# Two transformer blocks in one kernel: a 192-byte address step moved from the gated tile to the last low weight tile, and steps moved at the two feed-forward exits

## The chip, the cores and the metric

One core of a Trainium2 chip runs the whole program in one launch. The metric is the device time of one execution in microseconds, the median of several runs. Lower is better.

## What is computed

The reference chains two blocks on 256 tokens of width 1024, in float32.

```
# first block
h = x
h = h + 0.5 * swiglu(rmsnorm(h), ffn1_w1, ffn1_w3, ffn1_w2)      # inner width 2816
z = rmsnorm(h) @ w_in                                            # q, keys, values, gates, u
h = h + concat([nsa_attention(z...), s5_mixer(u...)]) @ w_out
h = h + 0.5 * swiglu(rmsnorm(h), ffn2_w1, ffn2_w3, ffn2_w2)
h = h + sigmoid(rmsnorm(h) @ w_ple_gate) * (p @ w_ple)
x = rmsnorm(h)
# second block, two layers, with 256 context tokens beside the 256 of x
for l in range(2):
    h, hc = modulated norms of x and ctx
    retention, chunk MLP and differential attention from h @ w_in[l]
    out = (sum of sigmoid(merge_logits) * (branch @ w_branch_out[l])) @ w_out[l]
    x = x + gate * rmsnorm(out)                                  # ctx likewise in layer 0
```

`s5_mixer` is a linear state-space scan; its tables of sines and cosines come from the parameters alone.

## The kernel before

Every engine has its program written out by hand, with semaphores between them. There is no scheduler: an engine does its steps in the order of the code.

**Weights.** They come in units of 128 x 1024 numbers (512 KB), in one stream, by SyncE's DMAs into a ring of four slots. A unit is used at nearly full precision in three passes on TensorE (PE). ScalarE (ACT) rounds it to `w_hi` (line 1329), VectorE (DVE) computes `w_lo = ring - w_hi` in `low_part` (line 478). Activations are split the same way, `hn_hi` and `hn_lo`, in the feed-forward parts also `hid_hi` and `hid_lo`. PE then does, for each of the eight 128-column tiles of a unit, `w_hi*x_hi` and `w_hi*x_lo` (`high_passes`, line 558), and after all eight tiles the eight `w_lo*x_hi` (`low_pass`, line 563). Where x is not ready in time the three stand together for each tile (`exact`, line 571). One such matmul moves 256 columns (512 in layer 0 of the second block, where context tokens ride along). The weight tile of the next matmul is loaded (PEld) while one runs.

**Addresses.** `w_lo` lies on the ring's own memory. Each slot has 128 numbers (`PLACE`) of room ahead of it, and `set_back` writes the split parts of some kinds of units 48 numbers (192 bytes) earlier. So for those units the weight tiles start at a multiple of 512 bytes, while `hn_hi` and `hn_lo` start 192 bytes past one. Units of other kinds have both at 192. The hidden tiles have four slots, f % 4: slot 0 of `hid_lo` starts at a multiple of 512 bytes, slots 1 to 3 are moved by `TILE_STEP` = 48 numbers (class `SteppedTiles`) and start 192 bytes past one, and so does every slot of `hid_hi`, which lies behind.

**A feed-forward part** (`ffn`, for `ffn1` and `ffn2`) has 22 steps f, each with a unit of w1, of w3 (`up`) and of w2 (`down`), in the order w1(f+1), w3(f+1), w2(f). The outputs of `down` build up in PSUM banks 0 to 3 over all f. Then PE waits at the exit: DVE adds the four banks to the residual `h` (line 2105), ACT squares the eight tiles of `h` (line 1311), PE sums the squares with a matrix of ones (`sumsq`, line 586, in float32), ACT takes the root (lines 1317 and 1318), DVE scales (line 1932), ACT rounds to `hn_hi` (line 1404), DVE makes `hn_lo` (line 1936), and the next products start.

**Filling work.** After `ffn1` PE has `lags` (line 694) and `turn_input` (line 683, eight transposes a call) for the state-space part; after `ffn2` it has `embedding` (line 984). DVE's `turn_tables` makes the arguments of the tables at f = 5 and 6 of `ffn1`. ACT takes their sines after `ffn1` (lines 1420 and 1421), loads the table of functions for the root (`root_table`, line 1306), and rounds two units. Modulation vectors are matrix-vector products on DVE, two halves of 1024 numbers each (`modulation`, lines 1958 and 1962), strewn over the program.

```
            root_table()
            high_parts(2)
            squares(1, h, resid_ready, [k // 2 + 1 for k in range(KT)])
            root(1, bank(7, 0, T), T, sumsq_ready, 2, D, rstd_ready)
            hn_high(1)
```

## Time and profile before

| | |
|---|---|
| median of 3 runs | 1483.34 us (1478.86 to 1489.1) |
| the profiled execution's own time | 1488.34 us |
| its span in the profile | 1486.6 us |
| PE, DVE, ACT busy | 97%, 64%, 49% of the span |
| PE's granted clock over the span | 0.996 of full |
| HBM read | 220.94 MB |

The profile is of one execution that took 5.0 us more than the median of the runs. The span is the time from the first to the last instruction, 1.74 us less than the execution's own time.

### The profile page before, as it was taken

The page shows a single profiled execution, that of the slowest core. Times are in us where ns is not written, and L with a number is a line of the kernel's source. Part 1 is how long each engine was busy: PE and PEld are TensorE (multiplying, and loading weights), DVE is VectorE, ACT ScalarE, POOL GpSimd, SP SyncE. Part 2 cuts the span into 40 slices and gives each one's busy share as a digit, 9 for nine tenths or more (in the row PEclk, how much of TensorE's full clock was granted, in tenths as well). Part 3 has the DMA queues.
Part 4 walks back from the last instruction along what each step waited for, and adds up shares of the span by engine and source line. Part 5 has one row for each costly group of instructions (what it writes and reads, how often), then busy time and mean ns, then how long its engine had stood idle before and what let it go on. Part 6 is the DMA issues. An engine that isn't in the chain of part 4 may idle for free.

```text
span 1486.6 us, 25861 instructions
## 1 busy us (share of the span) xinstructions
PE 1438.4 (97%) x9976; PEld 1283.5 (86%) x9976; DVE 957.2 (64%) x1516; ACT 721.2 (49%) x1252; POOL 95.7 (6%) x153
## 2 busy tenths in 40 slices
PE   6999999989999998999999999999999999999997
PEld 6999989769999998877778788888889887889997
DVE  5888779677666678865654447654246745646665
ACT  5444465366444466346445353222245446555444
POOL 4700000000000000102001000000000102010000
PEclk9999999999999999999999999999999999999999
DMA  7766645526766744642321224543333542335663
GB/s 279 248 212 202 220 132 197 172 70 232 227 214 221 229 154 152 190 153 78 86 83 60 71 72 156 170 127 114 101 112 100 156 124 83 100 93 184 206 211 130
DMA packets 72440, 227.43 MB, mean 153 GB/s; under 512 B 7072, under 2 KB 21408, under 8 KB 71840
## 3 DMA queue, kind: packets, MB, share of 16 engines
q1 hardware_dynamic: 54528, 194.67, 40.5%
q10 hardware_dynamic: 16416, 27.34, 5.7%
q0 software_dynamic: 1408, 4.20, 1.2%
q8 instruction: 61, 1.00, 0.3%
q14 instruction: 27, 0.22, 0.1%
HBM read 220.94 MB, written 1.05 MB: 149 GB/s over the span
## 4 chain that ended last, share of the span: by engine, by line
PE 83%; DVE 6%; DMA 5%; ACT 4%; issue 2%; SPq 0%; DVEq 0%; ACTq 0%
PE ps L558 33%; PE ps L571 21%; PE ps L563 17%; DMA ring<-stream 4%; DVE w_lo L478 2%; ACT w_hi L1329 2%; PE ps L586 2%; PE ps L1079 1%; PE ps L1095 1%; PE ps L1087 1%; PE ps L1163 1%; PE ps L1152 1%; PE ps L1132 0%; DMA pk<-pack 0%; PE ps L1112 0%
## 5 line engine op out<-in xcount | busy, mean ns | idle before, releaser
L478 DVE TENSOR_TENSOR w_lo<-ring,w_hi 128x1024 fp32r<-128x1024 f32 (+1 forms) x347 | 414.6, 1201 | 267.0 <-ACT w_hi L1329 262.6
L1329 ACT ACTIVATE w_hi<-ring 128x1024 fp32r<-128x1024 f32 (+1 forms) x347 | 360.5, 1040 | 325.1 <-DMA ring<-stream 245.9
L558 PE MATMUL ps<-hn_hi,w_hi 128*128 128x256 f32 (+1 forms) x1720 | 489.3, 315 | 3.6 <-ACT w_hi L1329 1.7
L558 PE MATMUL ps<-hn_lo,w_hi 128*128 128x256 f32 (+1 forms) x1720 | 480.4, 309 | 0.0
L558 PEld LDWEIGHTS ps<-hn_hi,w_hi 128*128 128x128 f32 x1720 | 323.5, 188 | 26.9 <-issue 5.3
L558 PEld LDWEIGHTS ps<-hn_lo,w_hi 128*128 128x128 f32 x1720 | 323.5, 188 | 19.4 <-issue 0.7
L563 PE MATMUL ps<-hn_hi,w_lo 128*128 128x256 f32 (+1 forms) x1720 | 288.5, 310 | 0.5 <-DVE w_lo L478 0.5
L563 PEld LDWEIGHTS ps<-hn_hi,w_lo 128*128 128x128 f32 x1720 | 244.7, 188 | 20.1 <-DVE w_lo L478 0.7
L1398 ACT ACTIVATE area<-ps 128x512 f32<-128x512 f32 (+1 forms) x136 | 67.1, 507 | 192.0 <-PE ps L563 177.9
L571 PE MATMUL ps<-area_r,w_hi 128*128 128x256 f32 (+1 forms) x578 | 132.3, 323 | 1.2 <-ACT area L1398 0.7
L571 PEld LDWEIGHTS ps<-area_r,w_hi 128*128 128x128 f32 x578 | 96.3, 189 | 10.8 <-DVE w_lo L478 0.9
L571 PE MATMUL ps<-area_r,w_lo 128*128 128x256 f32 (+1 forms) x289 | 93.0, 322 | 0.0
L558 PE MATMUL ps<-hid_hi,w_hi 128*128 128x256 f32 x352 | 83.2, 278 | 2.1 <-ACT w_hi L1329 1.3
L558 PE MATMUL ps<-hid_lo,w_hi 128*128 128x256 f32 x352 | 83.0, 278 | 0.0
L571 PE MATMUL ps<-w_hi,hn_hi 128*128 128x512 f32 (+1 forms) x192 | 77.1, 401 | 0.0
L571 PE MATMUL ps<-w_lo,hn_hi 128*128 128x512 f32 (+1 forms) x192 | 73.5, 383 | 0.0
L571 PE MATMUL ps<-w_hi,hn_lo 128*128 128x512 f32 (+1 forms) x192 | 73.2, 381 | 0.0
L558 PEld LDWEIGHTS ps<-hid_hi,w_hi 128*128 128x128 f32 x352 | 66.1, 188 | 2.6 <-ACT w_hi L1329 1.7
L558 PEld LDWEIGHTS ps<-hid_lo,w_hi 128*128 128x128 f32 x352 | 66.2, 188 | 0.0
L571 PE MATMUL ps<-hn_hi,w_hi 128*128 128x256 f32 (+1 forms) x175 | 55.6, 318 | 5.0 <-DVE hn_lo L1936 2.9
L571 PEld LDWEIGHTS ps<-area_r,w_lo 128*128 128x128 f32 x289 | 54.4, 188 | 4.4
L2800 POOL DMA_DIRECT2D area<-area x24 | 14.1, 595 | 683.1 <-ACT area L1398 683.1
(331 smaller groups left out, 1845.5 us busy)
## 6 DMA issues: line engine op xcount, KB each, us to landing
ring<-stream SPq DMA_DIRECT2D x359, 512.0 KB, 3.8
mod_at<-mod_stream ACTq DMA_DIRECT2D x24, 512.0 KB, 5.5
area<-mod_stream ACTq DMA_DIRECT2D x22, 512.0 KB, 4.7
area<-area POOLq DMA_DIRECT2D x16, 128.0 KB, 5.2
area<-area POOLq DMA_DIRECT2D x8, 256.0 KB, 4.0
pk<-pack ACTq DMA_DIRECT2D x1, 1610.0 KB, 7.3
pk<-pack SPq DMA_DIRECT2D x1, 1549.0 KB, 12.0
h<-x_in SPq DMA_DIRECT2D x1, 1024.0 KB, 4.8
```

Source lines behind the costliest of these rows:

```text
L478: eng.tensor_tensor(lo[:, 0:w], raw, hi[:, 0:w].bitcast(F32), ALU.subtract).then_inc(lo_ready[who], 1)
L558: m = pe.matmul(dst, weights[0][wcols], x[n][xcols], start=(start and n == 0), stop=False, skip_group_check=True)
L563: return pe.matmul(dst, weights[1][wcols], x[0][xcols], start=False, stop=stop, skip_group_check=True)
L571: m = pe.matmul(dst, w_, x_, start=(start and n == 0), stop=(stop and n == 2), skip_group_check=True)
L586: m = pe.matmul(bank(b, 0, tokens), c("ones"), src, start=(k == first), stop=(k == KT - 1), skip_group_check=True)
L1079: pe.matmul(bank(4 + m_, T * st, 2 * T - T * st), diffz[rows, 4 + hh, q0:q0 + P], diffz[rows, hh, keys], start=True, stop=True).then_inc(s ...
L1087: m = pe.transpose(bank(6, P * kt, P), aux[:, 4 + n % 2, P * kt:P * kt + P], c("ident"))
L1095: m = pe.matmul(bank(7, P * qt, P), diffv[:, kt, P * hh:P * hh + P], aux[:, 6 + n % 2, P * kt:P * kt + P], start=(kt == 2 * st), stop=(kt ...
L1152: m = pe.matmul(bank(4 + n % 2, T * kt, T), retz[:, hh, T * st + P * kt:T * st + P * kt + P], retz[:, 4 + hh, T * st:T * st + T], start=(k ...
L1163: m = pe.matmul(bank(6 + n % 2, 0, T), retv[:, 2 * st + kt, P * hh:P * hh + P], aux[:, n % 2, T * kt:T * kt + T], start=(kt == 0), stop=(s ...
L1329: act.activation(w_parts(name)[0][:, 0:w], ring[:, u % RING, PLACE:PLACE + w], ACT.Copy).then_inc(hi_ready, 1)
L1398: act.activation(dst, bank(BANK[name][0], 0, tokens), func, **kw).then_inc(act_evac, 1)
```

## The change

**The step.** The class `SteppedTiles` goes, and `hid_hi` and `hid_lo` change places, so that every hidden slot starts 192 bytes past a multiple of 512; everything behind them keeps its address. Instead `low_step` gives 48 numbers for chosen units: all 44 w2 units, units 0 and 4 of `wout` and of `pleg`, and in layer 1 of the second block units 0 and 2 of `dq`, `rq`, `dg`, `rg`, `mu`, `mg`, units 0, 2, 4 and 6 of `wo`, the 8 `mlog` units of branch 0 and the 8 wide `wbo` units. These are 80 units of 347. In such a unit the last of the eight `w_lo` tiles lies 192 bytes further on (`SteppedLow`), 192 past a multiple of 512 like the moving tile. The seven tiles ahead of it stay. DVE makes its `w_lo` in two instructions, of 896 and 128 columns; the second tells PE.

**The exits.** PE adds to a semaphore `bank_down` in the last low pass as banks 0, 1 and 2 are done, and DVE starts each of the first three residual additions on that; the fourth still waits for the whole unit. At `ffn1` the two copies of masks stand ahead of the additions; at `ffn2` one half of a modulation vector is moved behind them. `turn_input(0)` moves ahead of `sumsq(1)`. The two sines move into `ffn1`, to f = 9 and f = 11. Four semaphores become two (`dve_handed`, `act_handed`), with the same order of events.

```diff
@@ -21,7 +21,7 @@
 P = 128
 AREA = 25472
-AREA_SHIFT, TILE_STEP = 32, 48
+AREA_SHIFT = 80
 D = 1024
 KT = D // P
 T = 256
@@ -116,6 +116,31 @@
     return 0
+def low_step(name):
+
+    kind, l = name[0], name[1] if len(name) > 1 else 0
+    if kind in ("ffn1", "ffn2"):
+        return 48 if l == "w2" else 0
+    if kind in ("pleg", "wout"):
+        return 48 if name[1] % 4 == 0 else 0
+    if kind in ("dq", "rq", "dg", "rg", "mu", "mg", "wo") and l == 1:
+        return 48 if name[2] % 2 == 0 else 0
+    if kind in ("mlog", "wbo") and l == 1:
+        return 48 if name[2 if kind == "mlog" else 3] == 0 else 0
+    return 0
+
+
+class SteppedLow:
+
+    def __init__(self, rows, step):
+        self.rows, self.step = rows, step
+
+    def __getitem__(self, at):
+        p, cols = at
+        step = self.step if cols.start >= UW - P else 0
+        return self.rows[p, cols.start + step:cols.stop + step]
+
+
 UNIT_WIDTH = lambda name: BW if name[0] == "wbo" and name[3] == 1 else UW
 SPLIT_UNITS = [name for name in UNITS if name[0] in SPLIT_KINDS]
 SPLIT = {name: n for n, name in enumerate(SPLIT_UNITS)}
@@ -226,17 +251,6 @@
 SLOTS = [head_steps(l) for l in range(LAYERS)]
-class SteppedTiles:
-
-    def __init__(self, rows, width, step):
-        self.rows, self.width, self.step = rows, width, step
-
-    def __getitem__(self, at):
-        p, k, cols = at
-        begin = k * self.width + (self.step if k else 0)
-        return self.rows[p, begin:begin + self.width][:, cols]
-
-
 def two_block_kernel(nc, stream, mod_stream, cond, pack, pack2, bs_rows, x_in, ctx_in, out):
     with ExitStack() as es:
         def sb(name, shape, dt=F32):
@@ -284,10 +298,9 @@
         pgate = sb("pgate", [P, LAYERS, KT, 2])
         sb("area_shift", [P, AREA_SHIFT])
-        with nc.sbuf_tensor("hid_lo", [P, TILE_STEP + 4 * T], F32R) as hid_low, nc.sbuf_tensor("hid_hi", [P, 4, T], F32R) as hid_hi:
+        with nc.sbuf_tensor("hid_hi", [P, 4, T], F32R) as hid_hi, nc.sbuf_tensor("hid_lo", [P, 4, T], F32R) as hid_lo:
             pass
-        sb("tile_step", [P, TILE_STEP])
-        hid = [hid_hi, SteppedTiles(hid_low, T, TILE_STEP)]
+        hid = [hid_hi, hid_lo]
         with nc.sbuf_tensor("area_r", [P, AREA], F32R) as area_r:
             pass
         area = sb("area", [P, AREA])
@@ -466,7 +479,8 @@
         def w_parts(name):
             at = PLACE - set_back(name)
-            return w_hi[:, SPLIT[name] % HI, at:at + UW], w_lo[:, UNIT[name] % RING, at:at + UW]
+            lo = w_lo[:, UNIT[name] % RING, at:at + UW + low_step(name)]
+            return w_hi[:, SPLIT[name] % HI, at:at + UW], SteppedLow(lo, low_step(name))
         def low_part(eng, name, body=0):
@@ -475,7 +489,11 @@
             raw = ring[:, UNIT[name] % RING, PLACE:PLACE + w]
             hi, lo = w_parts(name)
             eng.wait_ge(hi_ready, SPLIT[name] + 1 + body)
-            eng.tensor_tensor(lo[:, 0:w], raw, hi[:, 0:w].bitcast(F32), ALU.subtract).then_inc(lo_ready[who], 1)
+            if low_step(name):
+                eng.tensor_tensor(lo[:, 0:w - P], raw[:, 0:w - P], hi[:, 0:w - P].bitcast(F32), ALU.subtract)
+                eng.tensor_tensor(lo[:, w - P:w], raw[:, w - P:w], hi[:, w - P:w].bitcast(F32), ALU.subtract).then_inc(lo_ready[who], 1)
+            else:
+                eng.tensor_tensor(lo[:, 0:w], raw, hi[:, 0:w].bitcast(F32), ALU.subtract).then_inc(lo_ready[who], 1)
         def load_mod(eng, m, body=0, first=False):
@@ -627,6 +645,8 @@
                     for j in range(KT):
                         m = low_pass(bank(j // 2, T * (j % 2), T), wt, (all_p, slice(P * j, P * j + P)),
                                      hid, (all_p, f % 4, all_t), f == FT - 1)
+                        if f == FT - 1 and j in (1, 3, 5):
+                            m.then_inc(s("bank_down"), 1)
                     m.then_inc(units_multiplied, 1)
                 first_up()
@@ -759,11 +779,11 @@
                                   hn, (all_p, k, slice(P * tt, P * tt + P)), k == 0, k == KT - 1, x_stationary=True)
                 m.then_inc(units_multiplied, 1)
+            turn_input(0)
             sumsq(1, T)
             pe.wait_ge(resid_ready, 1)
             pe.wait_ge(s("decay_ready"), 1)
             lags()
-            turn_input(0)
             pe.wait_ge(rstd_ready, 2)
             turn_input(1)
             project_pair([("u", 0), ("u", 1)], T, normed_ready, [NORMED[1] + k + 1 for k in range(KT)])
@@ -1377,6 +1397,11 @@
                             act.wait_ge(s("angle_ready"), 1)
                             act.activation(s5v[:, 7:9, :], s5v[:, 5:7, :], ACT.Sin, scale=TWO_PI).then_inc(s("angle_sin"), 1)
+                        if f == 9:
+                            act.wait_ge(s("turns_ready"), 1)
+                            act.activation(costab[:, :, :], costab[:, :, :], ACT.Sin, scale=TWO_PI)
+                        if f == 11:
+                            act.activation(sintab[:, :, :], sintab[:, :, :], ACT.Sin, scale=TWO_PI).then_inc(s("tables_ready"), 1)
                 else:
                     with act.Fori(0, (FT - 2) // 4) as it:
                         for f in range(1, 5):
@@ -1416,9 +1441,6 @@
             for st in range(2):
                 act.activation(cond_silu(st), cond_silu(st), ACT.Silu).then_inc(cs_ready, 1)
             ffn("ffn1", 0)
-            act.wait_ge(s("turns_ready"), 1)
-            act.activation(costab[:, :, :], costab[:, :, :], ACT.Sin, scale=TWO_PI)
-            act.activation(sintab[:, :, :], sintab[:, :, :], ACT.Sin, scale=TWO_PI).then_inc(s("tables_ready"), 1)
             root_table()
             high_parts(2)
             squares(1, h, resid_ready, [k // 2 + 1 for k in range(KT)])
@@ -2098,14 +2120,20 @@
                 if n == 0:
                     scan_decays()
                 else:
-                    modulation(LATE_MOD - 1)
-                product(dve, tag, "w2", FT - 1)
+                    modulation(LATE_MOD - 1, halves=(0,))
+                if n == 0:
+                    dve.tensor_copy(negc, c("causal")).then_inc(masks_ready, 1)
+                    dve.tensor_copy(idb, c("ident")).then_inc(masks_ready, 1)
                 for m in range(4):
+                    if m < 3:
+                        dve.wait_ge(s("bank_down"), 3 * n + m + 1)
+                    else:
+                        product(dve, tag, "w2", FT - 1)
                     hh = h[:, 2 * m:2 * m + 2, :].rearrange("p a b -> p (a b)")
                     stt(hh, bank(m), 0.5, hh, ALU.mult, ALU.add).then_inc(resid_ready, 1)
-            dve.memset(eps[:, :], EPS).then_inc(s("eps_set"), 1)
+            dve.memset(eps[:, :], EPS).then_inc(s("dve_handed"), 1)
             dve.wait_ge(consts_loaded, 16 * NC_DMAS)
             for k in range(1, KT, 2):
                 dve.wait_ge(squares_ready, k + 1)
@@ -2113,8 +2141,6 @@
             low_parts("ffn1", 0, 1)
             norm(0, "g_ffn1")
             ffn("ffn1", 0)
-            dve.tensor_copy(negc, c("causal")).then_inc(masks_ready, 1)
-            dve.tensor_copy(idb, c("ident")).then_inc(masks_ready, 1)
             low_until(("u", 1))
             norm(1, "g_mix")
@@ -2323,6 +2349,8 @@
             low_parts("ffn2", 0, 1)
             norm(2, "g_ffn2")
             ffn("ffn2", 1)
+            low_until(("pleg", 0))
+            modulation(LATE_MOD - 1, halves=(1,))
             low_until(("pleg", 1))
             norm(3, "g_ple")
 
```

End of `ffn1` on ACT, before (`area<-area` are the two sines, `area<-h` the squares) and then changed:

```order
L1354 ACTIVATE hid_hi<-area 128x256
L1329 ACTIVATE w_hi<-ring 128x1024
L1420 ACTIVATE area<-area 128x1024
L1421 ACTIVATE area<-area 128x1024
L1306 ACT_TABLE_LOAD
L1329 ACTIVATE w_hi<-ring 128x1024 x2
L1311 ACTIVATE area<-h 128x256 x8
L1317 ACTIVATE lnr<-ps,eps 128x256
L1318 ACTIVATE rstd<-lnr 128x256
```

```order
L1374 ACTIVATE hid_hi<-area 128x256
L1349 ACTIVATE w_hi<-ring 128x1024
L1326 ACT_TABLE_LOAD
L1349 ACTIVATE w_hi<-ring 128x1024 x2
L1331 ACTIVATE area<-h 128x256 x8
L1337 ACTIVATE lnr<-ps,eps 128x256
L1338 ACTIVATE rstd<-lnr 128x256
```

The sines are gone from between the last rounding and the table load.

End of `ffn1` on PE, before and changed (`area,pk` with 128x256 is `sumsq`, 32x96 is `lags`, `pk,area` is `turn_input`):

```order
L558 MATMUL ps<-hid_lo,w_hi 128x256
L563 MATMUL ps<-hid_hi,w_lo 128x256 x8
L586 MATMUL ps<-area,pk 128x256 x8
L694 MATMUL ps<-area 32x96 x32
L683 MATMUL ps<-pk,area 128x128 x16
L571 MATMUL ps<-hn_hi,w_hi 128x256
```

```order
L576 MATMUL ps<-hid_lo,w_hi 128x256
L581 MATMUL ps<-hid_hi,w_lo 128x256 x8
L703 MATMUL ps<-pk,area 128x128 x8
L604 MATMUL ps<-area,pk 128x256 x8
L714 MATMUL ps<-area 32x96 x32
L703 MATMUL ps<-pk,area 128x128 x8
L589 MATMUL ps<-hn_hi,w_hi 128x256
```

Eight transposes now stand ahead of the sum of squares.

End of `ffn2` on DVE, before and changed (`h<-ps,h` are the residual additions):

```order
L2048 TENSOR_TENSOR area<-area,ps 128x256
L2054 TENSOR_TENSOR hid_lo<-area,hid_hi 128x256
L478 TENSOR_TENSOR w_lo<-ring,w_hi 128x1024
L1958 SCALAR_TENSOR_TENSOR mod_junk,mods<-mod_at,cond_at 128x1024
L1962 SCALAR_TENSOR_TENSOR mod_at,mods<-mod_at,cond_at 128x4x256
L2105 SCALAR_TENSOR_TENSOR h<-ps,h 128x512 x4
L478 TENSOR_TENSOR w_lo<-ring,w_hi 128x1024 x2
```

```order
L2070 TENSOR_TENSOR area<-area,ps 128x256
L2076 TENSOR_TENSOR hid_lo<-area,hid_hi 128x256
L493 TENSOR_TENSOR w_lo<-ring,w_hi 128x896
L494 TENSOR_TENSOR w_lo<-ring,w_hi 128x128
L1980 SCALAR_TENSOR_TENSOR mod_junk,mods<-mod_at,cond_at 128x1024
L2133 SCALAR_TENSOR_TENSOR h<-ps,h 128x512 x4
L493 TENSOR_TENSOR w_lo<-ring,w_hi 128x896
L494 TENSOR_TENSOR w_lo<-ring,w_hi 128x128
L1984 SCALAR_TENSOR_TENSOR mod_at,mods<-mod_at,cond_at 128x4x256
L496 TENSOR_TENSOR w_lo<-ring,w_hi 128x1024
```

The second half of the modulation vector stands behind the additions and behind the first of the two `w_lo`, and split units have two rows.

## Rows read from the trace of the kernel before

**Rows 1.** Page: busy us of each engine, share of the span, instructions.

```profile
PE 1438.4 (97%) x9976; PEld 1283.5 (86%) x9976; DVE 957.2 (64%) x1516; ACT 721.2 (49%) x1252; POOL 95.7 (6%) x153
```

**Rows 2.** Page: the chain of work that ended last, by engine.

```profile
PE 83%; DVE 6%; DMA 5%; ACT 4%; issue 2%; SPq 0%; DVEq 0%; ACTq 0%
```

**Rows 3.** Timeline, end of `ffn1`: start us, duration us, engine, line, operation, [idle before].

```profile
199.54 1.04 ACT L1421 ACTIVATE area<-area 128x1024 f32<-128x1024 f32 x1
200.60 1.28 ACT L1306 ACT_TABLE_LOAD   x1
...
200.76 1.07 PE L563 MATMUL ps<-hid_hi,w_lo 128*128 128x256 f32 x8
201.87 2.48 DVE L2105 SCALAR_TENSOR_TENSOR h<-ps,h 128x512 f32<-128x512 f32 x4 [1.17 <-PE ps L563]
...
203.81 2.55 ACT L1311 ACTIVATE area<-h 128x256 f32<-128x256 f32 x8
204.26 5.41 PE L586 MATMUL ps<-area,pk 128*128 128x256 f32 x16 [2.43 <-ACT area L1311]
...
211.06 1.97 PE L683 MATMUL ps<-pk,area 128*128 128x128 f32 x16
212.78 0.37 PE L571 MATMUL ps<-hn_hi,w_hi 128*128 128x256 f32 x1
```

**Rows 4.** Windows: from:to, us, PE busy (x), granted clock, DMA share, GB/s.

```profile
204.90:208.20 3.30, 3.30 (x10) 0.50 0.06 22
```

**Rows 5.** Timeline, end of `ffn2`, all engines.

```profile
534.58 1.10 PE L563 MATMUL ps<-hid_hi,w_lo 128*128 128x256 f32 x8
...
534.98 1.22 DVE L1962 SCALAR_TENSOR_TENSOR mod_at<-mod_at,cond_at 128x1024 f32<-128x1024 f32 x1
...
536.13 2.48 DVE L2105 SCALAR_TENSOR_TENSOR h<-ps,h 128x512 f32<-128x512 f32 x4
536.85 2.56 ACT L1311 ACTIVATE area<-h 128x256 f32<-128x256 f32 x8 [1.93 <-DVE h L2105]
537.32 3.72 PE L586 MATMUL ps<-area,pk 128*128 128x256 f32 x16 [1.63 <-ACT area L1311]
...
540.87 3.62 PE L984 MATMUL ps<-pk,ring 128*128 128x256 f32 x16
...
544.14 0.47 PE L571 MATMUL ps<-hn_hi,w_hi 128*128 128x256 f32 x1
```

**Rows 6.** Timeline of ScalarE inside `ffn1`, around f = 9 and f = 11.

```profile
106.16 1.06 ACT L1329 ACTIVATE w_hi<-ring 128x1024 fp32r<-128x1024 f32 x1 [4.10 <-DMA ring<-stream]
...
120.82 1.07 ACT L1329 ACTIVATE w_hi<-ring 128x1024 fp32r<-128x1024 f32 x1 [1.94 <-DMA ring<-stream]
```

**Rows 7.** Windows, PE alone: one at 370; the last and the sum of seven others.

```profile
370.00:390.00 20.00, 20.00 (x179) 1.00 0.77 237
...
1386.00:1476.00 90.00, 89.94 (x765) 1.00 0.60 188
...
sum 174.00, PE 173.94; mean PE 24.85
```

**Rows 8.** Timeline of PE: `w2` units on hidden slots 0 and 1.

```profile
129.97 0.28 PE L558 MATMUL ps<-hid_hi,w_hi 128*128 128x256 f32 x1
...
131.85 1.08 PE L563 MATMUL ps<-hid_hi,w_lo 128*128 128x256 f32 x8
...
138.20 0.28 PE L558 MATMUL ps<-hid_hi,w_hi 128*128 128x256 f32 x1
...
140.01 1.07 PE L563 MATMUL ps<-hid_hi,w_lo 128*128 128x256 f32 x8
```

**Rows 9.** Groups of VectorE: xcount | busy us, mean ns | idle before.

```profile
L478 DVE TENSOR_TENSOR w_lo<-ring,w_hi 128x1024 fp32r<-128x1024 f32 x331 | 403.9, 1226 | 246.6 <-ACT w_hi L1329 242.2
...
L478 DVE TENSOR_TENSOR w_lo<-ring,w_hi 128x512 fp32r<-128x512 f32 x16 | 11.0, 689 | 20.4 <-ACT w_hi L1329 20.4
```

**Rows 10.** Waits of PE: us in total, times, longest us.

```profile
PE ps L563 <- DVE w_lo L478: 1.9, 4, 0.6
```

More of the change, by code:

```diff
@@ L1791, in _ @@
                     if l == 0 and slot == 4:
-                        act.activation(merge_cond(1), late_cond(1), ACT.Copy).then_inc(s("cond_moved"), 1)
+                        act.activation(merge_cond(1), late_cond(1), ACT.Copy).then_inc(s("act_handed"), 1)
                         act.wait_ge(s("mod_used"), MERGE_MOD)
@@ L2393, in _ @@
             low_until(("dk", 0, 1))
-            dve.wait_ge(s("final_square"), 1)
-            tt_(aux[:, 8, T:2 * T], bank(7, T, T), aux[:, 8, 0:T], ALU.mult).then_inc(s("final_mean"), 1)
+            dve.wait_ge(s("act_handed"), 1)
+            tt_(aux[:, 8, T:2 * T], bank(7, T, T), aux[:, 8, 0:T], ALU.mult).then_inc(s("dve_handed"), 1)
             dve.wait_ge(s("x_rstd"), 1)
```

8 lines of the change are left out of this document (4 added, 4 removed).

## The prediction

> **What bounds the kernel now.** I read the page first, then the chain of waits, then the timeline at the two exits of the feed-forward parts, then windows of PE alone. PE is busy 97% of the span, DVE 64% and ACT 49% [rows 1], and 83% of the chain that ended last is PE [rows 2]. So time can be won in two ways only: where PE stands still, and where its matmuls follow each other more slowly than they could.
>
> *Standing still.* The exit of `ffn1` [rows 3]: PE starts its last eight low matmuls at 200.76 and idles 2.43 us until 204.26. The wait names ACT's first square, and ACT is the late one: the second sine runs at 199.54 (1.04 us; the first, of the same size, just ahead of it), then the table load (1.28 us), two roundings (2.0 us; one is 1.06 in [rows 6]), and only at 203.81 the squares. DVE had begun its additions at 201.87. PE's sum of squares then takes 5.41 us. At the exit of `ffn2` the same 16 instructions go from 537.32 to 540.87 and a little more, some 3.6 us [rows 5]. The difference is the clock: from 204.90 to 208.20 it is granted at 0.50 [rows 4], the lower of its two levels (1.2 and 2.4 GHz), after PE had idled the 2.43 us.
>
> *Going slowly.* Matmuls of 256 columns come at two paces at the full clock. From 370 to 390 us 179 of them touch a window of 20 us; a matmul lasts 0.28 us, so some 2.5 are counted twice at the edges, and the spacing is 20.00 / 176.5 = 113.3 ns. From 1386 to 1476 it is 90.00 / 762.6 = 118.0 ns [rows 7]. I call these the tight and the wide pace. PE is never idle in either, and the instructions are the same. Read one after the other, the starts show that the wide pace begins behind a short wait or behind a change from the float32 matmuls and then persists over dozens of units. Seven such stretches (108 to 114.5, 424.5 to 463.5, 524 to 531, 553.5 to 560.5, 1206.5 to 1217, 1335 to 1349, 1386 to 1476) add up to 174 us [rows 7]. At the tight pace they would take 174 x (1 - 113.3/118.0) = 6.9 us less. The stretch from 424.5 passes one unit on hidden slot 0 at the wide pace and comes out tight behind the next such unit at 463.5; the one from 524 also ends behind one. So a tile at another address can throw PE back to the tight pace. It has a price where the pace is tight already: a `w2` unit on slot 0 needs 131.85 - 129.97 = 1.88 us for its 16 high matmuls, one on slot 1 140.01 - 138.20 = 1.81 us [rows 8].
>
> **The change part by part.** The sum is made against the profiled execution (1488.34 us), then carried to the median.
>
> *Exit of `ffn1`.* Without the sines ACT loads the table at 198.7, is through with it at 200.0 and with the two roundings at 202.0. The additions: bank 0 is done two low matmuls after 200.76, so with 0.28 us for a matmul at about 201.2; DVE has its copies of masks (0.4 us) out of the way by 201.1. Four additions of 0.62 us (2.48/4) would end at 203.7, not 204.35; the fourth may start at 201.85. The squares (2.55 us for eight) start at 202.0 and wait for the last bank: end 204.3, before 206.4. PE has eight transposes for the hole: half of the 16 in 1.97 us [rows 3], 0.95 us, from 201.9 to 202.8. The sum of squares starts there with squares waiting, and at the full clock takes 3.5 us [rows 5]: end 206.3, before 209.67. Behind it 1.4 us of `lags` (from the sum's end at 209.67 to 211.06) and the other 0.95 us of `turn_input` give 208.7; the norm is as far behind the sum as before, where the first product at 212.78 followed both almost without a gap. So it starts at about 209.0 and I take 3.8 us. Of these 1.7 are the clock (3.4 us at half), which hangs on PE no longer standing still; without that the term is 2.1. The term's range is 2.1 to 4.2.
>
> *Exit of `ffn2`.* DVE runs the second half of the modulation vector from 534.98, and the additions wait for it until 536.13, though PE is through at 535.7 [rows 5]. Changed, the first addition starts at about 535.0 and the first square at 535.7 in place of 536.85. ACT then squares without a break, 2.55 us, so the whole tail moves by 1.15 us: `embedding` from 540.87 to 539.7, the first product from 544.14 to 543.0. The moved half costs 1.22 us between the two `w_lo` of `pleg`; the second of these is needed with the first product, and DVE is free from 537.6 to the norm at 540.9: 1.15 + 1.22 + 1.2 us fill it to within 0.3 us. Term 1.15, range 0.5 to 1.3.
>
> *Sines inside `ffn1`.* Two of 1.05 us on ACT. They stand behind roundings where ACT idles 4.10 us (f = 9) and 1.94 us (f = 11) for the ring's next unit [rows 6]. That idle time covers them: 0. If a unit came early there, w_hi would be 1.05 us late against some 2.5 us that it is ahead; still 0.
>
> *The split `w_lo`.* 1024 columns take 1226 ns, 512 take 689 [rows 9]: 1.05 ns a column and 150 ns fixed, of which the next instruction hides some 80. So 0.07 to 0.15 us more for DVE in each of 80 units, 6 to 12 us on an engine with 36% to spare. On the path this counts only where PE waits for `w_lo`: 4 times on line 563, 1.9 us in all [rows 10], a few more behind the exits. Between 0.3 and 1.2 us, taken 0.5.
>
> *The step.* No row shows a single tile of this kind. From below: nothing, since the one other case, a whole unit's tiles at 192 against 0, costs 70 ns for 24 matmuls [rows 8], 3 ns each, so 80 single tiles with one or two disturbed neighbours cost 0.2 to 1.6 us; I take 0.6. The 12 units on slot 0 lose their 70 ns: 0.6 to 0.8 us won. These cancel. What matters is whether the tile ends a wide stretch. It recurs every 24 matmuls of a kind (every 8.2 us in the feed-forward parts, every few units in layer 1), where slot 0 came round every 33 us, and only there. The three longest stretches of the list (from 424.5, 1335 and 1386), 143 of the 174 us, lie among chosen units. Slot 0 worked on two of its three tries. If the single tile works as often, a stretch is cut to some 12 us, and about 80% of 6.9 is won: 5.5 us. Ends: 0 and 6.9.
>
> Here the Trainium skill speaks against this change. It says that PE has two read ports into SBUF, one for the moving and one for the stationary operand, so that loading the next weights takes nothing from a running matmul (TensorE: Matmul & The Clock Gate, "Step-by-step: what each phase is for"). By that rule an address step moves nothing at all, and the sum would end at the exits. The rows with two paces and with the slower slot 0 speak against so plain a reading, but they don't show that one tile is enough.
>
> Sum against the profiled execution: 3.8 + 1.15 + 5.5 - 0.5 = 9.95 us, 1478.4 us. That execution lies 5.0 us over the median, and since wide stretches start at chance waits, part of these 5.0 will be wide pace that the median run has less of. For the median I keep half of the pace term: 3.8 + 1.15 + 2.8 - 0.5 = 7.2, so **1476 us**.
>
> **The rivals.** *A, the forecast:* both exits and the release work, 1470 to 1481.
>
> *B, the step does nothing.* The exits give 5.0, the split takes 0.5, and without slot 0 a wide stretch in a feed-forward part has nothing to end it: the 40 us from 424.5 could run to the exit at 532, 70 us more at 4%, 2.7 us. 1478.9 to 1482, call it 1480. For it: one of three tries of a whole unit failed, and this is one tile.
>
> *C, more than the forecast.* The executions before hold as much wide pace as the profiled one, all of it goes, and the short waits shrink too: 3.8 + 1.3 + 6.9 + 2 = 14 us, 1469 or below.
>
> *D, the step throws PE out of the tight pace.* This ends on the other side. The tile at 192 over a moving tile at 192 is a disturbance in every chosen unit. If it leaves PE at the wide pace, all 256-column matmuls of those stretches go wide: 2 x 66 feed-forward units, 16 of `wout` and `pleg`, 56 units of layer 1, each 24, and 8 of 36, in all 5184 matmuls x 4.7 ns = 24.4 us, less the 6.9 that are wide already: +17.5, less the exits +12.5, 1496. It decides from 5.0 us / 4.7 ns = 1060 further matmuls at the wide pace. Against it: units on slot 0, disturbed 24 times over, left the pace tight each time it had been tight.
>
> *E, the exits don't give it.* The clock still falls at 205 (PE idles before the transposes are allowed, or the drop was earned before), or the gain waits behind the ring at the next projections. Exits 2.5, pace 2: 1479 to 1483.
>
> **How the numbers follow.** A 0.50, B 0.22, C 0.10, D 0.07, E 0.11. A measurement of this kernel can tell about 1% (15 us) from no change. Faster by over 1% is below 1468.5: most of C and the edge of A, 0.13. Slower by over 1% is above 1498: part of D, 0.02. The rest is 0.85. The range for 8 in 10 runs from the middle of C to the upper end of B: 1467 to 1483.
>
> **What would show it.** Right: no clock drop near 205 us and `sumsq` of 3.5 us there; first products some 3.8 us after PE's last low matmul less than before (12.0 us from 200.76 becomes 8.2), and 9.56 us from 534.58 becomes 8.4; windows of 256-column matmuls at 113 ns in layer 1 to the end. Wrong: a window of 118 ns that runs on over several chosen units (B), or begins at them (D); a PE that waits more often on `w_lo`. The forecast also fails if the median run held hardly any wide pace.

## The result, and the profile after

The change makes the kernel slower: 1493.02 us median of 6 runs (1492.22 to 1497.1) against 1482.62 us of 6 runs before (1478.86 to 1489.1), ratio 1.0064 with the 95% interval 1.0042 to 1.0086. The profiled execution took 1492.45 us, its span 1490.7; before they were 1488.34 and 1486.6. The forecast was 1476, with a range of 1467 to 1483.

The page of the changed kernel: busy us, share and instructions of each engine; the chain that ended last; one group (xcount | busy us, mean ns | idle before).

```profile
PE 1448.4 (97%) x9976; PEld 1294.9 (87%) x9976; DVE 963.6 (65%) x1596; ACT 722.7 (48%) x1252; POOL 96.7 (6%) x153
...
PE 87%; DVE 5%; ACT 3%; DMA 2%; issue 2%; SPq 0%; DVEq 0%; ACTq 0%
...
L493 DVE TENSOR_TENSOR w_lo<-ring,w_hi 128x896 fp32r<-128x896 f32 x80 | 87.2, 1091 | 57.4 <-ACT w_hi L1349 56.8
```

Against [rows 1] PE is busy 10 us more with the same 9976 instructions, and the chain holds 87% of PE where [rows 2] had 83%: less standing still, slower going. The split `w_lo` is there, 80 instructions more on VectorE.

The end of `ffn1`, timeline of all engines, to be laid beside [rows 3]:

```profile
202.52 1.28 ACT L1326 ACT_TABLE_LOAD   x1
202.53 1.09 DVE L493 TENSOR_TENSOR w_lo<-ring,w_hi 128x896 fp32r<-128x896 f32 x1 [0.52 <-ACT w_hi L1349]
...
203.54 0.28 DVE L494 TENSOR_TENSOR w_lo<-ring,w_hi 128x128 fp32r<-128x128 f32 x1
...
203.74 0.69 DVE L2045 COPY area<-area 128x1024 f32<-128x1024 f32 x1
...
204.77 1.11 PE L581 MATMUL ps<-hid_hi,w_lo 128*128 128x256 f32 x8
205.21 2.48 DVE L2133 SCALAR_TENSOR_TENSOR h<-ps,h 128x512 f32<-128x512 f32 x4 [0.37 <-PE ps L581]
...
205.71 1.03 PE L703 MATMUL ps<-pk,area 128*128 128x128 f32 x8
205.93 2.57 ACT L1331 ACTIVATE area<-h 128x256 f32<-128x256 f32 x8
...
206.59 3.62 PE L604 MATMUL ps<-area,pk 128*128 128x256 f32 x16
207.60 2.35 DVE L496 TENSOR_TENSOR w_lo<-ring,w_hi 128x1024 fp32r<-128x1024 f32 x2
...
212.96 0.36 PE L589 MATMUL ps<-hn_hi,w_hi 128*128 128x256 f32 x1 [0.28 <-DVE hn_lo L1958]
```

The sines are gone from here, `turn_input(0)` (L703) fills the hole, the squares and the sum follow at once. The sum of squares takes 3.62 us where it took 5.41, and the first product behind it starts at 212.96: 8.19 us after the last eight low matmuls began, where [rows 3] had 212.78 - 200.76 = 12.02. That is 3.83 us won; the forecast said 3.8.

The end of `ffn2`, beside [rows 5]:

```profile
538.80 1.11 PE L581 MATMUL ps<-hid_hi,w_lo 128*128 128x256 f32 x8
...
539.24 2.48 DVE L2133 SCALAR_TENSOR_TENSOR h<-ps,h 128x512 f32<-128x512 f32 x4 [0.23 <-PE ps L581]
539.96 2.57 ACT L1331 ACTIVATE area<-h 128x256 f32<-128x256 f32 x8 [0.27 <-DVE h L2133]
...
540.43 3.72 PE L604 MATMUL ps<-area,pk 128*128 128x256 f32 x16 [0.53 <-ACT area L1331]
...
542.84 1.22 DVE L1984 SCALAR_TENSOR_TENSOR mod_at<-mod_at,cond_at 128x1024 f32<-128x1024 f32 x1
...
543.99 3.62 PE L1004 MATMUL ps<-pk,ring 128*128 128x256 f32 x16
...
547.25 0.47 PE L589 MATMUL ps<-hn_hi,w_hi 128*128 128x256 f32 x1
```

From 538.80 to 547.25 are 8.45 us, where [rows 5] had 9.56: 1.11 us won, and 1.15 had been forecast. So both exits gave what they should, 4.9 us. The two profiled executions are 4.1 us apart the other way, so 4.9 + 4.1 = 9 us have been lost elsewhere.

Windows of PE alone in the changed kernel (from:to, us, PE busy (x), granted clock, DMA share, GB/s): inside `ffn1`, inside `ffn2`, two in layer 1, and the exit of `ffn1`.

```profile
40.00:200.00 160.00, 160.00 (x1361) 1.00 0.67 213
374.00:530.00 156.00, 156.00 (x1327) 1.00 0.67 216
1362.00:1386.00 24.00, 23.80 (x202) 1.00 0.64 206
1392.00:1446.00 54.00, 54.00 (x461) 1.00 0.64 204
202.40:208.00 5.60, 5.60 (x45) 1.00 0.57 179
```

The same four windows of the kernel before:

```profile
40.00:200.00 160.00, 158.61 (x1388) 1.00 0.67 216
374.00:530.00 156.00, 155.66 (x1355) 1.00 0.68 221
1362.00:1386.00 24.00, 23.56 (x207) 1.00 0.66 206
1392.00:1446.00 54.00, 54.00 (x461) 1.00 0.67 209
```

The last row of the changed kernel answers to [rows 4]: the clock stays at 1.00, its level of 2.4 GHz. In the four windows it is at that level too, with both kernels. But inside the MLPs PE now never waits and still gets through fewer matmuls, 1361 against 1388 and 1327 against 1355. The spacing in `ffn2` is 156.00 / (1327 - 2.5) = 117.8 ns, which is the wide pace, and it holds for the whole window. (From 1392 on both kernels are wide, the one before by chance.) The timeline of PE shows where it begins:

```profile
26.47 0.28 PE L576 MATMUL ps<-hn_hi,w_hi 128*128 128x256 f32 x1
...
28.28 1.07 PE L581 MATMUL ps<-hn_hi,w_lo 128*128 128x256 f32 x8
30.46 0.36 PE L576 MATMUL ps<-hid_hi,w_hi 128*128 128x256 f32 x1 [1.11 <-ACT w_hi L1349]
...
32.37 1.08 PE L581 MATMUL ps<-hid_hi,w_lo 128*128 128x256 f32 x8
33.28 0.28 PE L576 MATMUL ps<-hn_hi,w_hi 128*128 128x256 f32 x1
...
35.17 1.11 PE L581 MATMUL ps<-hn_hi,w_lo 128*128 128x256 f32 x8
```

The 16 high matmuls of an ordinary unit take 1.81 us up to 28.28, 113 ns each. There is a wait of 1.11 us, and the `w2` unit of f = 0 starts still at the tight pace. Its eight low matmuls begin at 32.37, and the last reads the moved tile. Their starts lie 113 or 114 ns apart up to that last one, and the next matmul starts 119 ns behind it. The next unit needs 35.17 - 33.28 = 1.89 us for the same 16 matmuls, 118 ns each. From there to the exit at 205 the starts of successive matmuls lie 117 to 119 ns apart. `ffn2` does the same from 366.4 on. In layer 1 the float32 block ends at 1354.6 with PE tight, it goes wide at the next chosen unit and, but for some matmuls behind a wait of 0.46 us at 1389.6, stays there until 1463.

To put a size on it I took the starts of all successive matmuls of 256 columns, left out the pairs whose spacing differs from 113.3 ns by 15 ns or more (waits and changes of operand), and added up spacing less 113.3 ns over the rest, some 5590 pairs. I call this sum the *excess* below; it is 0 for a kernel that is tight throughout. It is 9.10 us before and 21.77 us after: +12.7 us, of which 5.8 lie in `ffn1`, 4.4 in `ffn2` and 1.3 in layer 1. The balance of the two profiled executions, +4.1 us, is then: exits -4.9, excess +12.7, and -3.7 for the rest. Of that rest 2.4 us are idle time of PE (span less busy is 48.2 us before and 42.3 after, of which 3.5 belong to the exits), which fits a PE that asks for each unit later.

### The profile page after: what moved, and what is told of

It reads as the page before. It is cut to its first block, busy times and chain, and to the rows that moved or that the text cites. A ratio compares the mean times of both kernels' runs of the same rounds, so it can differ in the third digit from the quotient of the medians.

```text
span 1490.7 us, 25941 instructions
## 1 busy us (share of the span) xinstructions
PE 1448.4 (97%) x9976; PEld 1294.9 (87%) x9976; DVE 963.6 (65%) x1596; ACT 722.7 (48%) x1252; POOL 96.7 (6%) x153
## 4 chain that ended last, share of the span: by engine, by line
PE 87%; DVE 5%; ACT 3%; DMA 2%; issue 2%; SPq 0%; DVEq 0%; ACTq 0%
PE ps L576 37%; PE ps L589 20%; PE ps L581 18%; DMA ring<-stream 2%; PE ps L604 1%; PE ps L1099 1%; PE ps L1115 1%; ACT w_hi L1349 1%; PE ps L1107 1%; DVE w_lo L496 1%; PE ps L1183 1%; PE ps L1172 1%; PE ps L1152 0%; DMA pk<-pack 0%; PE ps L1132 0%
## 5 line engine op out<-in xcount | busy, mean ns | idle before, releaser
L576 PE MATMUL ps<-hn_hi,w_hi 128*128 128x256 f32 (+1 forms) x1720 | 494.6, 316 | 3.3 <-ACT area L1423 1.6
L576 PE MATMUL ps<-hn_lo,w_hi 128*128 128x256 f32 (+1 forms) x1720 | 486.0, 311 | 0.0
L496 DVE TENSOR_TENSOR w_lo<-ring,w_hi 128x1024 fp32r<-128x1024 f32 (+1 forms) x267 | 318.2, 1195 | 208.8 <-ACT w_hi L1349 205.5
L581 PE MATMUL ps<-hn_hi,w_lo 128*128 128x256 f32 (+1 forms) x1720 | 291.7, 312 | 0.3 <-DVE w_lo L496 0.3
L493 DVE TENSOR_TENSOR w_lo<-ring,w_hi 128x896 fp32r<-128x896 f32 x80 | 87.2, 1091 | 57.4 <-ACT w_hi L1349 56.8
L589 PE MATMUL ps<-hn_hi,w_hi 128*128 128x256 f32 (+1 forms) x175 | 56.1, 321 | 5.3 <-DVE hn_lo L1958 3.2
```

Source lines behind the costliest of these rows:

```text
L493: eng.tensor_tensor(lo[:, 0:w - P], raw[:, 0:w - P], hi[:, 0:w - P].bitcast(F32), ALU.subtract)
L496: eng.tensor_tensor(lo[:, 0:w], raw, hi[:, 0:w].bitcast(F32), ALU.subtract).then_inc(lo_ready[who], 1)
L576: m = pe.matmul(dst, weights[0][wcols], x[n][xcols], start=(start and n == 0), stop=False, skip_group_check=True)
L581: return pe.matmul(dst, weights[1][wcols], x[0][xcols], start=False, stop=stop, skip_group_check=True)
L589: m = pe.matmul(dst, w_, x_, start=(start and n == 0), stop=(stop and n == 2), skip_group_check=True)
```

## The experiments

Two theories stood at the start. **Pace:** the moved tile puts PE into the wide pace and holds it there; the rest of the change wins. **Split or slots:** the two-piece writing of `w_lo`, or the hidden slots' lost address step, costs the time. Each ratio below is to the kernel before, measured beside it on the same chip.

**e1_exits_only.** The change without the moved tile, hidden slots as before.

```diff
 def low_step(name):
+    return 0
...
-AREA_SHIFT = 80
+AREA_SHIFT, TILE_STEP = 32, 48
```

> The changed kernel without the low step (one instruction on DVE for each w_lo again) and with the hidden slots as before; all moves at the exits stay. Theory (the low tile at 192 bytes holds PE at the wide pace, and costs what the change lost): 1482.6 less 3.8 and 1.1 us at the exits, 1477.7 us, with 120 to 250 us of wide pace in the profile, no more than before. Rival (the moved sines, masks and semaphores cost inside ffn1): at or above 1490 us. The clock is not halved near 205 us in either.

**e2_step_only.** The kernel before with the moved tile and the hidden slots of the change, none of the moves at the exits.

> The kernel before with the low step and the swapped hidden tiles, and nothing of the moves at the exits. Theory: some 1482.6 + 15 = 1497 to 1499 us, wide pace through both feed-forward parts and layer 1 of the second block. Rival (step and exits hurt only together): 1483 us.

**e4_no_step_no_slots.** The change with `low_step` returning 0: no single tile moved, one instruction for `w_lo`, and all hidden slots at one address.

> The changed kernel without the low step, but with the hidden slots all at 192 bytes, so nothing in a feed-forward part disturbs PE. Theory: in ffn1 and ffn2 the pace after a wait is kept to the next wait; 12 units lose their 70 ns, so 1477 us, or up to 6 us more for each part in which a wait leaves the wide pace behind. Rival (slot 0 was what kept the pace tight): both parts wide throughout, 1489 us.

**e5_two_tiles.** As e4, but the tile is moved in two units of the whole kernel:

```diff
 def low_step(name):
-    if kind in ("ffn1", "ffn2"):
-        return 48 if l == "w2" else 0
+    return 48 if name in (("ffn1", "w2", 0), ("ffn2", "w2", 0)) else 0
```

> As e4, but with the low step in two units only, the w2 units of f = 0 of each feed-forward part: two tiles of 2776. Theory (one such tile takes PE out of the tight pace and nothing brings it back): 113 ns up to that tile, 118 ns from it to the exit, 2 x 1465 matmuls x 4.5 ns = 13 us over e4. Rival (each stepped tile has a price of its own, 80 of them 15 us): 0.4 us over e4.

Measured:

| kernel | median us (runs) | ratio, 95% interval | excess us, profiled | of it `ffn1`, `ffn2`, layer 1 |
|---|---|---|---|---|
| before | 1484.34 (24) | | 9.10 | 0.78, 2.20, 3.64 |
| e1_exits_only | 1480.15 (12) | 0.9973, 0.9960 to 0.9985 | 7.04 | 1.99, 0.75, 0.45 |
| e2_step_only | 1497.34 (6) | 1.0088, 1.0070 to 1.0105 | 22.04 | 6.69, 6.73, 4.94 |
| e4_no_step_no_slots | 1488.11 (12) | 1.0026, 1.0009 to 1.0042 | 15.74 | 6.66, 5.63, 0.85 |
| e5_two_tiles | 1490.63 (7) | 1.0042, 1.0026 to 1.0057 | 20.44 | 6.59, 6.60, 4.67 |
| the change | 1493.02 (6) | 1.0064, 1.0042 to 1.0086 | 21.77 | 6.59, 6.61, 4.95 |

The kernel before stood at 1484.34 us beside e1 to e5 and at 1482.62 beside the change, so the change is compared with them by its ratio. The exits are worth 4.2 us on the median (1484.34 to 1480.15), where e1's theory had 4.9. The change lies 0.0024 or 3.6 us under e2, which lacks them; the two intervals overlap, so this second figure only agrees with the first. The step and the slots are worth the other way: e2 has only these two and is 13 us slower than the kernel before. In its profile both MLPs go wide behind the wait ahead of f = 0 (at 30.1 and 367.9 us), before the first moved tile is read, and stay so.

Windows of PE in `ffn1`, `ffn2` and layer 1, e1_exits_only and then e4_no_step_no_slots:

```profile
40.00:200.00 160.00, 159.32 (x1389) 1.00 0.66 215
374.00:530.00 156.00, 156.00 (x1375) 1.00 0.70 225
...
1392.00:1446.00 54.00, 54.00 (x479) 1.00 0.69 214
```

```profile
40.00:200.00 160.00, 159.29 (x1353) 1.00 0.66 212
374.00:530.00 156.00, 156.00 (x1336) 1.00 0.68 219
...
1392.00:1446.00 54.00, 54.00 (x479) 1.00 0.72 218
```

e1 runs `ffn2` tight (156.00 / 1372.5 = 113.7 ns), e4 mostly wide. In e4 the wide pace began by itself, in `ffn1` behind a wait of 0.87 us that ended at 29.7 us, and in `ffn2` at 400.4 us, where one matmul starts 20 ns late and the profile shows no wait. It ran both times to the exit (205.9 and 539.7). In e1 three stretches that began as well ended at a `w2` unit on hidden slot 0 (at 62.7, 161.9 and 497.0 us). So the slots that the change straightens were what kept the MLPs (the two feed-forward parts) tight, as the rival of e4's expectation had it. Losing them costs 15.74 - 7.04 = 8.7 us of excess and 8.0 us of the median. e4's twelve runs spread from 1483.06 to 1492.15 us, so not every execution need be as wide as the profiled one.

The moved tiles then cost the rest, 0.0038 of the time or 5.6 us by the ratios of e4 and the change. Two of them, in e5, cost 2.5 us on the median where 13 had been expected, since e4's MLPs are wide already; the intervals of e4 and e5 overlap, so here the time decides nothing. Nor does the excess: of the 4.7 us by which e5's exceeds e4's, 3.8 lie in layer 1, where e5 has no moved tile. What shows the tile at work is the trace. In e5, as in the change, PE is back at 113 ns behind its wait at 28 us, goes wide at the matmul that reads the moved tile (31.4 us) and stays so to the exit. e5's windows are those of the change, to the matmul:

```profile
40.00:200.00 160.00, 160.00 (x1361) 1.00 0.66 212
374.00:530.00 156.00, 156.00 (x1327) 1.00 0.66 217
```

One tile, read for one matmul, sets the pace of the next 1465. That speaks against the split as a cause: in e5 it happens twice in the whole kernel. The direct test, the split without the address, wasn't run: at one address the second piece would write what the first still reads, unless VectorE waits between them as in e12 below. Nor was the moved tile run with the hidden slots as before, which could show whether slot 0 undoes it.

**Which addresses do it?** By the program's addresses ordinary weight tiles start at a multiple of 512 bytes and the moving tiles 192 beyond one. The moved tile is at 192, the position of the moving tiles. Three kernels, based on e5 so that each MLP starts wide, put one `w_hi` tile of each `w2` unit from f = 1 elsewhere; ScalarE and VectorE work in two pieces there.

```diff
+HIGH_STEP = {'ffn1': 16, 'ffn2': 32}   # e6, e7; e8: 48, 64 (numbers of 4 bytes)
+HIGH_FIRST = False                     # e6; e7, e8: True
...
+        at = self.at
+        if self.step and HIGH_FIRST and cols.stop <= P:
+            at -= self.step
+        if self.step and not HIGH_FIRST and cols.start >= UW - P:
+            at += self.step
+        return self.slots[p, self.slot, at + cols.start:at + cols.stop]
```

> Base is e5_two_tiles: the low step at w2 of f = 0 of each of the two MLPs holds PE at the wide pace (117.5 to 118 ns for one 256-column matmul) to the end of that MLP. Added: in every w2 unit from f = 1 the eighth tile of w_hi stands 64 bytes further in ffn1 and 128 bytes further in ffn2. Theory 1 (the pace is a state: one tile at some address sets it, another at some other address ends it, as the disturbing hidden slot 0 does in the kernel before): if one of the two distances is an ending one, the spacing of matmuls goes back to 113.3 ns in that MLP at the first such tile and 1465 matmuls times 4.4 ns, 6.4 us, are saved of the MLP (1484 us for one, 1478 for both). Rival (only a wait of PE or the end of the w_lo disturbance ends it, no address of a w_hi tile does): both MLPs stay at 117.5 to 118 ns, 1490 to 1492 us.

> As e6_high_last_64_128, but it is the first tile of w_hi that stands 64 bytes earlier in ffn1 and 128 bytes earlier in ffn2, in every w2 unit from f = 1. Theory 1 (some address of one tile ends the wide pace): 113.3 ns from the first such unit in the MLP where it does, 6.4 us less for each, 1478 to 1484 us. Rival (no address of a w_hi tile ends it): 117.5 to 118 ns to the end of both MLPs, 1490 to 1492 us.

> As e7_high_first_448_384, with the first tile of w_hi 192 bytes earlier in ffn1 and 256 bytes earlier in ffn2. Theory 1: 113.3 ns from the first such unit in the MLP where the address ends the wide pace, 6.4 us less for each, 1478 to 1484 us. Rival: 117.5 to 118 ns to the end of both MLPs, 1490 to 1492 us.

One profiled execution each: 1481.29, 1490.02 and 1491.05 us, beside 1483.6 of the kernel before. Theory 1 had 1478 to 1484 us for each. e6 is there; e7 and e8 are not, though e7's `ffn2` is mostly tight, because the rest of e7 stays wide (excess 15.13 us against 20.44 in e5) and its clock fell more often (see below). The timeline of PE in e6, where `ffn2`'s eighth `w_hi` tile (128 bytes further) is read at 371.6:

```profile
369.99 0.28 PE L609 MATMUL ps<-hid_hi,w_hi 128*128 128x256 f32 x1
...
371.88 1.07 PE L614 MATMUL ps<-hid_hi,w_lo 128*128 128x256 f32 x8
372.79 0.28 PE L609 MATMUL ps<-hn_hi,w_hi 128*128 128x256 f32 x1
...
374.60 1.07 PE L614 MATMUL ps<-hn_hi,w_lo 128*128 128x256 f32 x8
```

The 16 matmuls up to 371.88 take 1.89 us, those up to 374.60 take 1.81: wide before the tile, tight behind it. The same window of `ffn2` as above, in e7_high_first_448_384, holds 1369 matmuls where e5's has 1327:

```profile
374.00:530.00 156.00, 156.00 (x1369) 1.00 0.69 223
```

**e10_low_64_128** does this with the tile that the change moves, the eighth of `w_lo`.

> As e6_high_last_64_128, but it is the eighth tile of w_lo, the tile that the change moves, that stands 64 bytes further in ffn1 and 128 bytes further in ffn2 in the w2 units from f = 1 (192 bytes at f = 0, as in e5_two_tiles). Theory 1 (what counts is the address of a weight tile, whichever part it holds): ffn1 changes pace at each such tile, about half of it at 117.5 to 118 ns, and ffn2 is at 113.3 ns from its first such tile on, 1481 to 1485 us. Rival (only a tile of w_hi, which follows a unit's sixteen passes, can end the wide pace): both MLPs stay at 117.5 to 118 ns to their ends, 1490 to 1492 us.

1480.61 us, profiled, 0.4 us under the range of theory 1: `ffn2` did as it says, `ffn1` went tight at its second such tile and did not change to and fro. With all four kernels and the change, what one tile does (position counted from a multiple of 256 bytes; the moving tiles are at 192):

| tile moved by, bytes | position mod 256 | where | pace behind it |
|---|---|---|---|
| `w_lo` last, +192 | 192 | change, e2, e5 | wide, from either pace (e2 was wide already) |
| `w_hi` first, -64 | 192 | e7 `ffn1` | wide; after a wait at 91 us had freed PE, wide again at the next such tile (97.6) |
| `w_hi` last, +128 | 128 | e6 `ffn2` | tight, from either |
| `w_hi` first, -128 | 128 | e7 `ffn2` | tight at 374 and 481 us, missed at 473 |
| `w_lo` last, +128 | 128 | e10 `ffn2` | tight at 370 and 502 us, missed at 493 |
| `w_hi` last, +64; first, -192 | 64 | e6, e8 `ffn1` | the other pace, at every such tile |
| `w_lo` last, +64 | 64 | e10 `ffn1` | missed at 41 us, tight from 49 on, with some 20 ns lost at each tile |
| `w_hi` first, -256 | 0 | e8 `ffn2` | unchanged: wide to the exit (never met the tight pace) |

Counted over e6, e7 and e10 and the three kernels below, a tile at 128 met the wide pace in an MLP 16 times without a wait beside it. Twelve times PE was tight behind it. Four times it was not (e7 at 473 us, e10 at 493, e11 at 369, e12 at 428), and then the next such tile did it.

Theory 1 of the expectations holds, and more narrowly than it was put. In e7 -64 bytes in `ffn1` did not end the wide pace and -128 in `ffn2` did, in e8 -192 changed it back and forth and -256 did nothing: distances that agree modulo 256 agree in what they do, for every one of the tiles with one exception (64 in `w_hi` against `w_lo`).

**Can it be used?** Three kernels keep the exits and aim at the tight pace.

e9_high_128: no `w_lo` step, the eighth `w_hi` tile at +128 from f = 1 in both MLPs (`HIGH_STEP = {'ffn1': 32, 'ffn2': 32}`). e11_high_128_layer1: the same in layer 1 as well. e12_change_128: the change itself with another number in all four places, and a wait of VectorE for its own first piece, which was not run by itself:

```diff
-        return 48 if l == "w2" else 0
+        return 32 if l == "w2" else 0
...
+                ...subtract).then_inc(s("low_piece"), 3)
+                eng.wait_ge(s("low_piece"), low_count(name) + body)
```

> The change with its low step taken out (no disturbing hidden slot either) and, in the w2 units from f = 1 of both MLPs, the eighth tile of w_hi 128 bytes further. In e6_high_last_64_128 such a tile in ffn2 brought matmuls that were at 117.5 to 118 ns back to 113.3 ns at that very tile, and left those at 113.3 ns there. Theory 1 (it does so always): at most the first up and down units of each MLP are wide, so the time is the profiled 1481.3 us of e6 less the wide half of its ffn1 (some 750 matmuls times 4.4 ns, 3.3 us): 1477 to 1479 us in a profiled execution, against the kernel before 0.993 to 0.996. Rival 1 (the release in e6 came only out of the state that its captured tile made, and matmuls that go wide after a wait of PE are not brought back): ffn1 or ffn2 wide to its end as without any step, 1486 to 1488 us. Rival 2 (the two-piece writing on ScalarE and VectorE makes PE wait at the units): the trace shows waits of PE ahead of w2 units of 0.3 us or more, twice 15 of them, 1484 us or more.

> As e9_high_128, and the same 128 bytes for the eighth w_hi tile in layer 1 too: every second unit of six of its kinds of projection (dq, dg, rq, rg, mu, mg, wo) and one mlog unit in three. Theory 1: where layer 1 goes wide by chance, as it did from 1362 to 1460 us in e5_two_tiles, it comes back at the next such tile; against e9_high_128 equal when that one is tight in layer 1 anyway, up to 3.6 us (833 matmuls times 4.4 ns) less when it is not. Rival (the pieces cost more than the pace there gives): 0.2 us of ScalarE and VectorE for each of about 20 units come to the end as waits of PE, 1 to 4 us slower than e9_high_128.

> The whole change with one number altered: its stepped low tiles stand 128 bytes further instead of 192, in the same units of both MLPs, of pleg and wout and of layer 1 (VectorE waits between the two pieces for its own first piece, which the smaller distance needs). In e10_low_64_128 such a tile brought matmuls at 117.5 to 118 ns back to 113.3 ns. Theory 1 (the loss of the change is the address of 192 bytes and nothing else in it): both MLPs and layer 1 at 113.3 ns nearly throughout, 12.7 us less excess than the change's own profile, and the ratio to the kernel before becomes that of e1_exits_only or less, 0.995 to 0.998. Rival 1 (the change loses by its split writing of w_lo or its unstepped hidden slots, whatever the distance): 1.003 to 1.007, as the change itself and e4_no_step_no_slots. Rival 2 (layer 1 answers otherwise than the MLPs): MLPs at 113.3 ns and layer 1 at 117.5 to 118 ns from 1355 us to its end, 0.999 to 1.001.

| kernel | median us (12 runs each), before beside it | ratio, 95% interval | profiled us | excess us | of it `ffn1`, `ffn2`, layer 1 |
|---|---|---|---|---|---|
| e9_high_128 | 1481.17, 1484.96 | 0.9980, 0.9965 to 0.9994 | 1477.21 | 5.99 | 0.41, 0.54, 1.43 |
| e11_high_128_layer1 | 1480.61, 1484.96 | 0.9971, 0.9958 to 0.9984 | 1478.59 | 4.90 | 0.43, 0.86, 1.08 |
| e12_change_128 | 1480.84, 1483.67 | 0.9988, 0.9974 to 1.0002 | 1479.75 | 4.32 | 0.19, 0.94, 0.42 |

e12's windows, beside those of the change:

```profile
40.00:200.00 160.00, 159.70 (x1407) 1.00 0.68 219
374.00:530.00 156.00, 155.47 (x1360) 1.00 0.68 222
1362.00:1386.00 24.00, 24.00 (x214) 1.00 0.69 215
1392.00:1446.00 54.00, 53.37 (x471) 1.00 0.69 212
```

1407 matmuls where the change had 1361, 1360 in 155.47 busy us where it had 1327 in 156, 214 and 471 where it had 202 and 461. One number, 128 in place of 192 bytes, takes the excess from 21.77 to 4.32 us (in the two MLPs from 13.2 to 1.1) and the profiled time from 1492.45 to 1479.75; the ratios 0.9988 and 1.0064 lie well apart. VectorE's added wait can only make `w_lo` later. So the position of the tile decides: at 128 the same split and the same straightened slots lose nothing that shows, since the tile then does what slot 0 did. Rival 1 of that expectation falls. Layer 1 proves less against rival 2 than its windows suggest. Without any moved tile there, its excess was 3.6 to 4.8 us in five profiles (before, e5, e7, e8, e10) and 0.5 to 1.4 in four (e1, e4, e6, e9), so e12's 0.42 may be chance too.

Two expectations missed in size. e12's ratio came out above 0.995 to 0.998 and e9's above 0.993 to 0.996, and none of e9, e11 and e12 is told apart from e1_exits_only (0.9973), though their profiles hold 1.1, 2.1 and 2.7 us less excess. (e11 is no better than e9 either, which its theory allowed.) The waits of PE (us in total, times, longest), e12 first, then e1:

```profile
PE ps L583 <- ACT w_hi L1356: 2.9, 4, 0.9
```

```profile
PE ps L589 <- ACT w_hi L1362: 1.0, 3, 0.5
```

A PE at the tight pace asks sooner for units that ScalarE and the ring bring no sooner. But the sum of all idle time of PE (span less busy) is 45.0 us in e12 and 45.3 in e1, so that isn't where the gain went. Two kinds of chance do show. One is layer 1, as said: in e10 it was wide from 1354 to 1450, which is 3.7 us. The other is the clock. Behind some waits of PE the granted clock falls to 0.50 for 3.4 us, which loses 1.7 us. Two of these waits are in all thirteen profiles, but the drop is not: behind the one of 2.07 us near 305 it is there in seven, behind the one of 1.84 us near 583 in eight. e1's profile has four such drops ahead of the end and was the slowest of its twelve runs (1484.07 us). Those of e9, e11 and e12 have one each, e7's three, e5's one. Windows of PE in e1_exits_only behind a wait of 2.14 us at 241.1, and in e2_step_only, which keeps the hole at the exit of `ffn1`, behind its wait of 2.20 us there:

```profile
241.10:244.50 3.40, 3.40 (x16) 0.50 0.03 10
```

```profile
209.30:212.50 3.20, 3.20 (x9) 0.50 0.03 9
```

e9's 12 runs spread over 9.1 us, e11's over 5.3. How much of the missing gain these two explain stays open. The lowest ratios are those of e11 and e1, 0.3% under the kernel before; e9 and e12 are not told apart from them.

## Why the prediction was wrong

**The exits: right.** 3.8 and 1.15 us were forecast, 3.83 and 1.11 read off the timelines, and e1 gives 4.2 us of the median. The clock's part was right as well: no drop at 205 us, and the sum of squares in 3.62 us. None of the eleven profiles with the transposes in the hole has a drop there, and both without them (before, e2) do. Rival E is out.

**The split: right in kind.** Pieces of 896 and 128 columns take 1.09 and 0.28 us. In the timeline of `ffn1`'s end the instruction behind such a pair starts 1.21 us after the pair's first (202.53 to 203.74). Two whole ones take 2.35 us (207.60), so the second starts some 1.13 us after the first: 0.08 us for the split, and the forecast said 0.07 to 0.15. Waits of PE for `w_lo` did not grow:

```profile
PE ps L589 <- DVE w_lo L494: 0.6, 2, 0.5
...
PE ps L581 <- DVE w_lo L496: 0.3, 1, 0.3
```

0.9 us in all against 1.9 on line 563 in [rows 10], which fits a PE that is slower. The 0.5 us of the sum was not needed.

**The step: wrong, in sign.** This is the step of the prediction that failed. The forecast put its local cost at ±0 and its gain at 5.5 us ("If the single tile works as often, a stretch is cut to some 12 us"). Together with the straightened slots it cost 12.7 us of excess: the tile at 192 turned a tight PE wide (in the change and in e5 at the first one of each MLP) and never released one, while the same tile at 128 (e12) left 4.32 us of excess in place of 21.77. What failed is the likeness on which this rests: slot 0 in the kernel before moves the *moving* tile to another position than usual, the change moves a *weight* tile onto the position of the moving ones. That both are "192 bytes" said nothing. The rows held no weight tile at that position, and the text said so ("No row shows a single tile of this kind"), then took the chance that it releases from another kind all the same.

Rival D had the mechanism: all 5184 matmuls of the chosen stretches wide, 24.4 us of wide pace in all. Measured are 21.8 us in the whole kernel. It took off only the 6.9 us of the seven listed stretches, where the whole kernel before held 9.1 us of excess. With that it would have given 1483.3 + 24.4 - 9.1 - 5.0 = 1493.6, beside the measured median of 1493.02. That it fits so closely is luck: the 24.4 us are 2.6 too many, and the 3.7 us less of waits aren't in it. Its reason against, that units on slot 0 "left the pace tight each time it had been tight", is the same wrong likeness, and 0.07 was the price of it.

**Slot 0: sized too low.** Rival B put what the straightened slots lose at 2.7 us, one stretch that runs on. e4 shows 8.0 us of the median. Without slot 0 only another wait can end a wide stretch in an MLP, and in the profiled execution each MLP got one that ran to its exit. The forecast itself had no term for this loss; it left the releasing to the moved tile.

**The rule of the Trainium skill** that the prediction weighed (TensorE: Matmul & The Clock Gate, "Step-by-step: what each phase is for": two read ports, so that loading the next weights takes nothing from a running matmul) would have made the step worth nothing. e5, e6 and e12 speak against it as a rule for time: where one weight tile stands in SBUF changed the spacing of all matmuls behind it by 4%.

## What to carry to other kernels

A stretch in which an engine is never idle can still run at two speeds: divide a window by its count of matmuls before calling it bound. Where a state persists, ask of each edit both whether it can end the state and whether it can begin it, and price the second by all the work in reach; a disturbance that is known to end it in one arrangement of operands says nothing of another. And before an address is chosen for its effect, try its neighbours: here 128 bytes did what 192 was to do.
